# Feed-forward gate and up on one Trainium2 core: the high weights stream past high and low rows in one 512-column product, and VectorE adds the two halves

## The reference

```python
def conv_ffn(h, w_up, conv_w, conv_b, w_down):        # first two
    u = h @ w_up                                      # 1024 -> 2 * 2816
    u = depthwise causal convolution over 3 rows of u, + conv_b
    gate, val = jnp.split(u, 2, axis=-1)
    return (jax.nn.silu(gate) * val) @ w_down

def swiglu(h, w_gate, w_up, w_down):                  # the third
    return (jax.nn.silu(h @ w_gate) * (h @ w_up)) @ w_down
```

## Time and profile before

| | |
|---|---|
| runs (3) | median 1657.31 us, 1653.99 to 1659.87 |
| span of the profiled execution, first to last instruction | 1658.8 us |
| TensorE, products: busy | 1607.8 us, 97% |
| TensorE, weight loads: busy | 1430.8 us, 86% |
| VectorE busy | 1167.6 us, 70% |
| ScalarE busy | 964.3 us, 58% |
| gate and up products, L1670 | 3168 of 128x256, 22.8% of the chain that ended last |
| down products, L1689 | 792 of 128x512, 10.9% of that chain |
| DMA | 204 GB/s over the span, 183 to 185 in the feed-forward stages |

### The profile page before, as it was taken

The page is one execution under the profiler, slowest core; times in us unless marked ns, Lnnn a source line. Parts: engine busy times, 40 slices in busy tenths (PEclk is TensorE's granted clock), DMA queues, the critical chain, the costliest instruction groups (busy, mean ns, idle before and its releaser), DMA issues.

```text
span 1658.8 us, 30055 instructions
## 1 busy us (share of the span) xinstructions
PE 1607.8 (97%) x11794; PEld 1430.8 (86%) x11794; DVE 1167.6 (70%) x1347; ACT 964.3 (58%) x1258; POOL 26.5 (2%) x37
## 2 busy tenths in 40 slices
PE   7999999999989999999999999999999999999998
PEld 6988999899879999899889998998778888888886
DVE  5677667654557666786764545877569888988887
ACT  6566554555555554753454435734547777777775
POOL 0000000000000000110000000200000000000000
PEclk9999999999999999999999999999899999999999
DMA  7534554534415455352245544631339999999994
GB/s 263 184 127 178 180 198 180 178 131 175 153 51 204 180 193 183 140 184 93 77 178 190 190 178 152 185 119 62 153 136 372 347 352 364 356 362 354 353 367 157
DMA packets 48529, 339.15 MB, mean 204 GB/s; under 512 B 5824, under 2 KB 6000, under 8 KB 8496
## 3 DMA queue, kind: packets, MB, share of 16 engines
q1 hardware_dynamic: 46368, 330.94, 54.0%
q0 software_dynamic: 2064, 6.83, 1.4%
HBM read 336.66 MB, written 1.10 MB: 204 GB/s over the span
## 4 chain that ended last, share of the span: by engine, by line
PE 87%; DVE 6%; ACT 5%; issue 1%; DMA 1%; SPq 0%; DVEq 0%; ACTq 0%
PE PS L1670 23%; PE PS L831 17%; PE PS L1571 16%; PE PS L1689 11%; PE PS L1589 8%; PE PS L1220 2%; DVE MWL L2541 1%; PE PS L910 1%; ACT MWH L1836 1%; PE PS L1532 1%; DVE ARENA L2924 1%; PE PS L1620 1%; ACT HN L1765 1%; PE PS L1554 1%; DMA W<-in_weights 1%
## 5 line engine op out<-in xcount | busy, mean ns | idle before, releaser
L3131 DVE TENSOR_TENSOR EWL<-W,EWH 128x2048 fp32r<-128x2048 f32 x144 | 329.1, 2290 | 46.0 <-ACT EWH L2309 46.0
L2309 ACT ACTIVATE EWH<-W 128x2048 fp32r<-128x2048 f32 x144 | 276.2, 1919 | 67.2 <-PE PS L1589 36.9
L1670 PE MATMUL PS<-HTH,WH 128*128 128x256 f32 x1056 | 298.5, 283 | 4.5 <-DVE HTL L2507 4.5
L2536 DVE TENSOR_TENSOR WL<-W,WH 128x2048 fp32r<-128x2048 f32 x99 | 226.6, 2289 | 104.4 <-ACT WH L1818 103.6
L1670 PE MATMUL PS<-HTH,WL 128*128 128x256 f32 x1056 | 298.0, 282 | 0.0
L1670 PE MATMUL PS<-HTL,WH 128*128 128x256 f32 x1056 | 298.0, 282 | 0.0
L2541 DVE TENSOR_TENSOR MWL<-W,MWH 128x1024 fp32r<-128x1024 f32 x138 | 173.9, 1265 | 122.4 <-ACT MWH L1836 120.0
L1836 ACT ACTIVATE MWH<-W 128x1024 fp32r<-128x1024 f32 x138 | 144.6, 1055 | 167.7 <-PE PS L831 167.7
L1818 ACT ACTIVATE WH<-W 128x2048 fp32r<-128x2048 f32 x99 | 189.3, 1915 | 60.2 <-PE PS L1670 32.7
L1670 PEld LDWEIGHTS PS<-HTH,WH 128*128 128x128 f32 x1056 | 200.3, 190 | 6.2 <-issue 5.1
L1670 PEld LDWEIGHTS PS<-HTL,WH 128*128 128x128 f32 x1056 | 200.6, 190 | 1.1
(11 more groups left out here) (344 smaller groups left out, 2802.2 us busy)
## 6 DMA issues: line engine op xcount, KB each, us to landing
W<-in_weights SPq DMA_DIRECT2D x312, 1024.0 KB, 4.8
ARENA<-rows_m POOLq DMA_DIRECT2D x8, 192.0 KB, 5.8
ARENA<-rows_m POOLq DMA_DIRECT2D x2, 768.0 KB, 10.2
CS<-in_consts POOLq DMA_DIRECT2D x3, 403.0 KB, 4.3
X<-in_x SPq DMA_DIRECT2D x2, 512.0 KB, 3.9
out<-X SPq DMA_DIRECT2D x4, 256.0 KB, 2.8
PR<-in_params SPq DMA_DIRECT2D x1, 830.0 KB, 7.9
CS<-in_consts POOLq DMA_DIRECT2D x2, 403.5 KB, 4.5
```

The lines of the kernel that those rows point to most:

```text
L1670: ins = mm(PS[b][:, c * 256:(c + 1) * 256], wt[:, sl, o:o + P], ht[:, kk, :], start=(kk == 0 and n == 0), stop=(kk == KC - 1 and n == 2))
L2309: A(EWH[tile % SPLIT][:, :], tile_ap(w0 + tile), ACT.Copy).then_inc(sem("moe_hi"), 1)
L2536: TT(WL[:, j % SPLIT, :], tile_ap(t), WH[:, j % SPLIT, :].bitcast(F32), SUB).then_inc(lo_done, 2)
L3131: TT(EWL[tile % SPLIT][:, :], tile_ap(w0 + tile), EWH[tile % SPLIT][:, :].bitcast(F32), SUB).then_inc(sem("moe_lo"), 1)
```

## The change

HTH and HTL become the two halves of one tensor HTB. In `up` each unit has a bank of its own, 4 + 2 * half + c, in every group. Per chunk there is one 512-column product of WH with HTH and HTL side by side (`HTB[:, :, kk, :]`, columns 0 to 255 and 256 to 511 of the bank), and one 256-column product of WL with HTH added into columns 0 to 255. VectorE joins the halves: it copies columns 256 to 511 to a new SBUF tile U and adds columns 0 to 255 to it, once per unit; a new semaphore tells it that the first unit of a tile is done. ScalarE and VectorE then read U instead of the bank. In the glu stage the order on VectorE changes to join, `lo`, join, gate product, `lo`. The bank is given back by the addition. The split slots WH and WL move 2048 words up in their area to make room for U.

```diff
-    HT = nc.alloc_sbuf_tensor("HT", [P, KC, S], F32)
-    HTL = nc.alloc_sbuf_tensor("HTL", [P, KC, S], F32R)
+    HTB = nc.alloc_sbuf_tensor("HTB", [P, 2, KC, S], F32R)
+    HTH, HTL = HTB[:, 0], HTB[:, 1]
...
+    ff.U = a(2 * 1024).rearrange("p (b h c t) -> p b h c t", b=2, h=2, c=2)
...
# TensorE, up
-                    b, sl = 4 + 2 * (gs % 2) + half, j % SPLIT
+                    sl = j % SPLIT
                     await_split(j, i)
...
                     for c in range(2):
+                        b = 4 + 2 * half + c
+                        pe.wait_ge(free[b], k0[b] + gs + body * i)
                         for kk in range(KC):
...
-                            for n, (wt, ht) in enumerate(((WH, HTH), (WH, HTL), (WL, HTH))):
-                                ins = mm(PS[b][:, c * 256:(c + 1) * 256], wt[:, sl, o:o + P], ht[:, kk, :],
-                                         start=(kk == 0 and n == 0), stop=(kk == KC - 1 and n == 2))
-                    ins.then_inc(w_used, 1)
+                            mm(PS[b][:, :], WH[:, sl, o:o + P], HTB[:, :, kk, :], start=(kk == 0), stop=False, skip_group_check=True)
+                            ins = mm(PS[b][:, 0:256], WL[:, sl, o:o + P], HTH[:, kk, :], start=False, stop=(kk == KC - 1),
+                                     skip_group_check=True)
+                        ins.then_inc(w_used if c else sem(name + "_unit"), 1)
...
# ScalarE, group
+            def await_units(half, gs, i):
+                for b in (4 + 2 * half, 5 + 2 * half):
+                    act.wait_ge(free[b], k0[b] + gs + 1 + body * i)
...
-                            ins = A(dst[:, hb, c, :], PS[b + half][:, c * 256:(c + 1) * 256], ACT.Identity, scale=col(2), bias=col(3))
+                            ins = A(dst[:, hb, c, :], ff.U[:, hb, half, c, :], ACT.Identity, scale=col(2), bias=col(3))
...
# VectorE, group
+            def joined(half, gs, i, first):
+                for c in range(2):
+                    b = 4 + 2 * half + c
+                    if c:
+                        dve.wait_ge(w_used, w0 + (half if first else 3 * gs - 1 + half) + 1 + 3 * body * i)
+                    else:
+                        dve.wait_ge(sem(name + "_unit"), 2 * gs + half + 1 + 2 * body * i)
+                    dve.tensor_copy(ff.U[:, gs % 2, half, c, :], PS[b][:, 256:512]).then_inc(sem(name + "_lo_half"), 1)
+                    dve.wait_ge(sem(name + "_lo_half"), 4 * gs + 2 * half + c + 1 + 4 * body * i)
+                    TT(ff.U[:, gs % 2, half, c, :], ff.U[:, gs % 2, half, c, :], PS[b][:, 0:256], ADD).then_inc(free[b], 1)
...
                     for half, Y in enumerate((ff.YG, ff.YV)):
+                        joined(half, gs, i, first)
                         dve.wait_ge(sc, 3 * gs + 1 + half + 3 * body * i)
...
-                                ins = STT(Y[:, hb, c, s:256], PS[b + half][:, c * 256:c * 256 + 256 - s], w, Y[:, hb, c, s:256], MUL, ADD)
+                                STT(Y[:, hb, c, s:256], ff.U[:, hb, half, c, 0:256 - s], w, Y[:, hb, c, s:256], MUL, ADD).then_inc(sv, 1)
```

More of the change, by code:

```diff
@@ L164, in build @@
     arena_at = nc.sbuf_base - 4 * ARENA_N
-    HTH = nc.alloc_sbuf_tensor_at("HTH", [P, KC, S], F32R, offset=ht_at)
+    HT = nc.alloc_sbuf_tensor_at("HT", [P, KC, S], F32, offset=ht_at)
     MWH = nc.alloc_sbuf_tensor_at("MWH", [P, SPLIT, HALF], F32R, offset=mw_at)
@@ L170, in build @@
     assert 2 * SPLIT * HALF <= (RING - RAW) * KC * TW
-    ff_n = 4 * 2 * 512
+    ff_n = 6 * 2 * 512
     gh_n, wh_n = 2 * 512, SPLIT * KC * TW
@@ L430, in plan_ffn @@
         ffn_k0[n] = list(n_use)
-        for g in range(groups):
-            n_use[4 + 2 * (g % 2)] += 1
-            n_use[5 + 2 * (g % 2)] += 1
+        for b in range(4, 8):
+            n_use[b] += groups
         plan_y(n, BASE[n] + 3 * groups - 1)
@@ L2387, in split @@
                     hi(name, j, i)
+            def await_units(half, gs, i):
+                for b in (4 + 2 * half, 5 + 2 * half):
+                    act.wait_ge(free[b], k0[b] + gs + 1 + body * i)
             def group(gs, i, first=False):
[L2391 to L2394, removed]
+                hb = gs % 2
                 if kind != "conv":
[L2396 to L2400, removed]
+                    await_units(0, gs, i)
+                    A(f(ff.SG[:, hb]), f(ff.U[:, hb, 0]), ACT.Silu).then_inc(sc, 1)
+                    split(0 + (3 if first else 3 * gs + 2), i)
+                    split(1 + (3 if first else 3 * gs + 2), i)
+                    act.wait_ge(sv, gs + 1 + body * i)
                 else:
                     if gs >= 2:
-                        act.wait_ge(sv, 7 * (gs - 1) + 7 * body * i)
+                        act.wait_ge(sv, 9 * (gs - 1) + 9 * body * i)
                     off = PRM["conv0" if name == "ffn0" else "conv1"][0]
                     for half, dst in enumerate((ff.YG, ff.YV)):
-                        if half:
-                            act.wait_ge(w_used, w0 + j + 2 + dt)
+                        await_units(half, gs, i)
                         for c in range(2):
@@ L3226, in group @@
                             if s == 2:
-                                dve.wait_ge(sv, n0 + 2 + 3 * half)
+                                dve.wait_ge(sv, n0 + 2 + 4 * half)
                             for c in range(2):
@@ L3230, in group @@
                                 w = PR[:, col:col + 1] if isinstance(i, int) else PR[:, bass.ds(8 * body * i + col, 1)]
[L3231 to L3238 removed]
+                                STT(Y[:, hb, c, s:256], ff.U[:, hb, half, c, 0:256 - s], w, Y[:, hb, c, s:256], MUL, ADD).then_inc(sv, 1)
+                        split(j + half, i)
+                    dve.wait_ge(sv, n0 + 8)
                     dve.wait_ge(sc, 3 * gs + 3 + 3 * body * i)
@@ L3244, in group @@
                 if not first:
-                    split(j + 5, i)
+                    split(3 * gs + 4, i)
             group(0, 0, True)
```

41 lines of the change are left out of this document (15 added, 26 removed).

## The result

The changed kernel took 1729.97 us in the median (four runs, 1724.63 to 1731.07), the kernel before 1658.59 us (the three runs of its table and one more): a ratio of 1.0426, with a 95% interval of 1.0411 to 1.0441. It is slower by 71.4 us, where I had put 58.7. The profiled execution is the shortest of the four, 1724.63 us with a span of 1722.8.

A forecast was written before the change was run, and what follows sets the result against it. TensorE's order bounds the kernel before; VectorE's loop with its ScalarE trips would bound ffn0 and ffn1. +30.2 (ffn0), +31.3 (ffn1) and -2.8 (ffn2) make +58.7 us on the median 1657.3: 1716 us, range 1697 to 1742.

The forecast's parts named there:

- The bound and the sign: ffn0 and ffn1: VectorE's loop with trips to ScalarE becomes the bound, 19.39 us a group; slower, 0.93.
- The room: Convolution stages before the change: VectorE's loop with its waits takes 15.81 us against 16.85 a group, leaving 1.04 us.
- rival (1): All three stages: TensorE stays the bound everywhere, -8.2 us, 1649 us, faster; chance 5%.
- The join: VectorE: copy and addition for two units take 1.64 us, twice a group in the convolution stages.
- Hand-over and Identity: Each half of a convolution group: 0.10 us hand-over, then ScalarE's Identity pair and trip back to the taps, 1.22 us.
- Slots, registers and counters change nothing in time: Whole change: moved slots, register steps and counters were taken to add no time.
- The tail: End of ffn0 and ffn1: last group 13.7 us, then the last down projection 5.6 us.
- Rival (4): ffn0 and ffn1: TensorE's pauses in each group bring half clock, up to +12 us, 1728 us; chance 5%.
- The gated stage: ffn2: TensorE stays the bound at 16.60 us a group, VectorE's loop takes 13.9; saving 2.8 us.
- the unknowns: Uncertain sizes: copy -7 us, waiting instruction +10, hand-overs +2, Identity +5, two-run product -2.7 to +2.8 in ffn2.
- (2): 512-column product in all three stages: a two-run moving operand streams at half rate, 1875 us; chance 5%.
- (3): 512-column product: no cheaper than two of 256, so ffn2 saves nothing, 1719 us; chance 10%.

The follow-up runs named there:

- e7_after_again: The changed kernel run once more, nothing altered, beside the kernel with filled tails: 1728.69 us.
- e2: The changed kernel with each join cut to one copy, the low rows' sum left out of the result: 1688.98 us, ratio 1.019.
- e3: The changed kernel with the 512-column product split again into two of 256, joins and banks kept: 1731.9 us, ratio 1.0444.
- e8: The changed kernel with ScalarE's WH ahead of each Identity pair and VectorE's WL directly behind each join in the convolution stages: 1658.70 us, ratio 0.9999.
- e10: The kernel of e8 run once more, nothing altered: 1656.38 us, ratio 0.9991.
- e6: The changed kernel with 30 unread 512-column products ahead of the last down projection of each convolution stage: 1724.11 us.
- e9: The kernel of e8 with 10 unread 512-column products ahead of the last down projection of each convolution stage: 1655.81 us, ratio 0.9989.

## Why the prediction was right, and by how much off

**The bound and the sign** were right, and the runs show the mechanism: half of the join takes 0.43 us a step, the products give nothing in the convolution stages, the order alone takes the loss away.

**The room** of 1.04 us a group was the right thing to compare with. The changed kernel's VectorE is busy for 14.54 us of 19.76 and sets the pace all the same; rival (1) rested on such a share and fell.

**The join**, 1.64 us: 1.665. The copy of 256 columns, taken as 0.42, took 0.418; copy to addition waits 0.034 us, addition to the next copy starts 0.08 us before the end, as the earlier trace rows had it. By the sentence of the Trainium skill (VectorE: DVE Perf Modes, The DRAIN you can't avoid) that a semaphore after each step costs nothing the join would have been 1.42; here the trace differs, by 0.11 us for each waiting step.

**Hand-over and Identity.** I took 0.10 + 1.22 = 1.32 us a half. In the first two groups and the last it was 0.10 to 0.12 and 1.13. In the eight groups of the hardware loop it was 0.17 to 0.25 and 1.24 to 1.27: 1.50 in the first half and 1.41 in the second of the group shown. The groups written out are 19.43 us apart (predicted 19.39), those in the loop 19.77. The records show what is between, for ScalarE's Identity line and VectorE's tap line in all of the changed kernel, and the Identity line in the kernel before (count: duration in ns min/median/max, first and last start in us):

```profile
L2412 ACTq FUSED_REGOPS  x64: 74/74/83, 186.8 to 718.0; - x64
L3243 DVEq FUSED_REGOPS  x128: 57/57/81, 188.1 to 720.3; - x128
L2412 ACTq FUSED_REGOPS  x64: 74/74/83, 177.8 to 652.3; - x64
```

These are register steps, four a group on ScalarE and eight on VectorE, in the 16 groups of the two loops and in none outside: they compute the columns of scale and bias from the loop's index. In the group shown ScalarE's first stands at 226.3 us, behind the join's end. The kernel before has as many, but ScalarE's stood there while it waited for TensorE (2.76 us in the earlier trace rows); now they lie in the round trip. From the end of the Identity pair to the taps it is 0.03 us in the groups written out and 0.14 to 0.17 in the loop, which the earlier trace rows had already (0.15).

The step that failed is "Slots, registers and counters change nothing in time", and the term that it leaves too small is the hand-over: 0.24 + 0.17 for twice 0.10 is 0.21 of the 0.38 us by which a loop group passes my 19.39. The join (0.05), Identity (0.06) and the taps (0.04) are most of the rest. Eight groups at 0.38 us are 3.0 us in each stage. That the register steps are the cause is an inference from where they stand; no run took them out.

That the groups written out came within 0.04 us of 19.39 is partly luck. Their round trip is 1.22 us for my 1.32, and the taps take 1.88 us up to WL for my 1.80, since WL waits for ScalarE's WH there (in the last group WH ends at 347.88 us and WL starts at 347.98); I had written that it finds WH ready. The two errors cancel.

**The tail.** I summed the last group (13.7 us, measured 13.8) and added 5.6 us for the last down projection. The last one took 7.24 us with its hand-over, since the clock fell in the idle 8.2 us ahead of it; with that pause filled the 24 products took 5.7. Rival (4) looked for the clock within the groups, where TensorE's pauses of 1.2 to 1.7 us (start to start) left it at 1.00. It overlooked the end of the stage, where TensorE has done its last up and down projections while VectorE and ScalarE still need most of their last 13.7 us, and where nothing hides the cost. The nearest row of before, the 8.10 us on which rival (4) drew:

```profile
134.00:142.10 8.10, 4.97 (x30) 3.74 (x28) 5.66 (x12) 6.09 (x19) 0.00 (x0) 1.00 0.52 195
```

It stands ahead of the 3.40 us at 0.50 in the earlier trace rows; the tail had less work than that.

**ffn0 summed up.** The start is 0.1 us late, the groups take 3.1 us more than predicted, the last group 0.1 and the last down projection 1.6: 222.03 us where 217.2 were predicted. ffn1 missed by the same terms (groups 2.8, last down 1.6).

**The gated stage**, -2.8 us: at full clock 185.5 to 182.9, -2.6. Its groups took 16.57 us for a predicted 16.60. The other 1.5 us of its measured -4.0 is the half clock that the profiled execution of before had for 3.4 us from 842.0 us on and this one had not. ffn0 of before had such a stretch at its start too. The loop of 13.9 us that I had put for VectorE shows once: the second group starts its joins at 930.12 us and the third at 944.07, 13.95 us later, before TensorE's pace takes over.

**The number.** The measured change of 71.4 us is 12.7 over my 58.7. In the profiled executions the two convolution stages are 9.5 us over their prediction (in each some 3 from the groups, 1.6 from the tail), the gated stage is 1.2 and the rest of the kernel 2.9 under it: 64.0 us. The last 7.4 us are no part of that sum. The profiled execution is the shortest of four and the other three lie 4 to 6 us above it, at a granted clock of 0.986 to 0.988 instead of 0.992, while the profiled span of before, 1658.8, stands a little over its median. So the profile misses a part of the time at half clock that the median has; e7_after_again, profiled at 0.989 with a span of 1728.4, shows such a part (10.2 us in one tail, 3.4 more between ffn0 and ffn1). For the other runs no trace was kept, and where theirs lies stays open.

The range holds the result, though its ends don't come out of its terms exactly: the unknowns alone give 1696 to 1736, with rival (4) 1748, and not 1742.

Rivals (2) and (3) are out: pair and product took 0.346 and 0.229 us, where two products of 256 take 0.235. What the Trainium skill (Advanced Engine Details and Errata, Memory Cachelines) says of non-contiguous patterns in PSUM no run here shows; a moving operand of two runs in SBUF costs 2 ns a product or less.

## What to carry to other kernels

Ask of an engine that isn't the bound how long its own queue takes with every wait for a partner in it, and put that, not its busy share, against the bound; a step with a round trip in front of it costs its full length there. Where such a queue becomes the bound, look for order before work: putting an independent step into the wait gave back 70 us here that the same steps in the old order cost. And give each stage of a kernel its own answer: this edit gains in the gated stage, where VectorE's loop with its waits for ScalarE (13.95 us) stays under TensorE's 16.57, and loses in the two where it doesn't.

## What the hardware showed that I had not expected

- A moving operand of two runs of 256 columns, 8 KB apart, streams in 0.229 us for 512 columns, where one run takes 0.227.
- The granted clock fell to 0.50 for 6.8 to 10.2 us in all eight tails in which TensorE stood still for 6.4 to 8.3 us (the changed kernel twice, e2, e3), and in one of four tails with a pause of 2.57 us (e8, e10); with the pause filled it stayed at 1.00 in all four (e6, e9).
- Register steps of 74 ns stand in front of a ScalarE instruction with columns from a register, and of 57 ns in front of VectorE's, only inside a hardware loop. Groups there are 0.34 us longer than the same groups written out, once the steps stand in a round trip; that the steps are the cause is inferred.
- Identity of 256 columns takes 0.595 us from SBUF; where I had added 0.05 us a pair against PSUM, the pair took 1.10 us from SBUF and 1.02 from PSUM, 0.08 us more.
